# Turning the attention probabilities with plain products against a scaled diagonal

## The chip, the cores and the metric

One Trainium2 chip; the program runs on one of its cores. The metric is the device time of one execution in microseconds (us), here the median of the timed runs.

## The reference

The model is two transformer blocks over 512 latent and 256 context tokens of width 1024, everything in float32. What the change touches are its two attentions. Both compute softmax(scale · Q Kᵀ) V per head:

```python
def attend(q, k, v):                       # first block (MLA): 8 heads, 512 queries, 768 keys, value width 128
    s = jnp.einsum('bqhd,bkhd->bhqk', q, k).astype(F32) * MLA_SCALE
    p = jax.nn.softmax(s, axis=-1).astype(v.dtype)
    return jnp.einsum('bhqk,bkhd->bqhd', p, v)

# second block (GQA): 8 query heads in 2 groups, 512 queries, 512 keys, head width 64
scores = jnp.einsum('bqkgd,bskd->bkgqs', qblk, k).astype(jnp.float32) * scale
p = jax.nn.softmax(scores, axis=-1).astype(v.dtype)
return jnp.einsum('bkgqs,bskd->bqkgd', p, v)
```

## The kernel before

The program is a row of stages (`build`, from L3796). Each stage is a block with one instruction stream for each engine; the engines meet through semaphores, and the next stage starts when all are through. The stages with the attentions are reached from `mla` (call at L2662: 8 heads, key segments of 256 and 512, so 768 keys) and from `second_mixer` (call at L3247: 8 heads, 512 keys). They are called the MLA attention and the GQA attention below.

Float32 products are mostly made in three passes (`three_passes`, L300 to L305; L303, L304 and L305 are the three matmuls): each operand is held as a rounded high part and a low part, both of the type float32r, and high·high, high·low and low·high are added up in PSUM. A plain float32 product (`nc.tensor.matmul` on float32 operands) is one instruction in the source.

`attention` (L2271) serves both calls. Its work is cut into 32 units u = (head h, query block a of 128 queries), all written out (no loop on the engines). For a unit:

- TensorE, `score(u)`, L2316: scores of 128 queries against all keys, into a PSUM score bank. MLA: 10 matmuls (5 with 256 and 5 with 512 keys); GQA: 3 matmuls of 512 keys with 64 rows (the head width).
- VectorE, `find_peak(u)`: the row maximum (L2393) and its product with minus the scale (L2394).
- ScalarE, `raise_(u)`, L2359: exp of the scores, from PSUM into the buffer `probs` in SBUF, with the row sum as a by-product.
- VectorE: reciprocal of the row sum (L2412), then the whole probability tile times that share, in place (L2413), which releases `normed`.
- TensorE, L2342: each block of 128 queries x 128 keys is transposed against the identity `ident` into a PSUM bank (6 blocks in MLA, 4 in GQA), which releases `t_done`.
- ScalarE, `high(u)`, L2366: rounds the turned tile into a high part; VectorE, `low(u)`, L2399: the rest, which releases `t_kept`.
- TensorE, `value(m, part)`, L2328 (the matmuls are recorded at L303 to L305): probabilities times values for a pair of units; one half of the key blocks goes behind each unit (9 matmuls a unit in MLA, 6 in GQA, each 256 wide).
- ScalarE L2371 and VectorE L2405 split the output of a pair.

The order on each engine is the order in the source. TensorE, for every u: score(u+2); wait for `normed` of u; wait for `t_kept` of the unit that used the turn bank before; the transpositions of u; then half a `value` of the pair before. VectorE, for every u: wait for `raised` of u, L2412, L2413, low(u-1), every second time out_low, find_peak(u+2). ScalarE: high(u-1), every second time out_high, raise_(u+1). There are two `probs` buffers; MLA has 2 score banks and 1 turn bank (L2661), GQA has 3 score banks and 2 turn banks (L3246). Neither attention moves any data by DMA.

`k.row` is a scratch row of 768 words per partition; `stats` takes its words 0 to 31, and the GQA side keeps `steps` in words 704 to 767.

Of the kernel before, what the change touches and what calls it, by code (L numbers as in the profile page):

```python
# [28 lines left out]
ALU = mybir.AluOpType  # L29
AX = mybir.AxisListType  # L30

P = 128
# [267 lines left out]
def three_passes(k, out, stationary, moving, start, stop, **more):  # L300

    (sh, sl), (mh, ml) = stationary, moving
    k.nc.tensor.matmul(out, sh, mh, start=start, stop=False, **more)  # L303
    k.nc.tensor.matmul(out, sh, ml, start=False, stop=False, **more)  # L304
    return k.nc.tensor.matmul(out, sl, mh, start=False, stop=stop, **more)  # L305
# [1965 lines left out]
def attention(k, heads, key_segs, products_of, value_of, out_rows, dst_of, scale, rooms):  # L2271

    nc = k.nc
    k.stage()
    lo = key_segs[0][0]
    width = T - lo
    tiles = width // P
    stats = k.row[:, 0:32].rearrange("p (b c) -> p b c", c=4)  # L2280
    units = [(h, a) for h in range(heads) for a in range(4)]
    n_units, n_pairs, ahead = len(units), len(units) // 2, rooms.ahead
    probs, turned = rooms.probs, rooms.turned
    n_probs, n_scores, n_turns = len(probs), len(rooms.score_banks), len(rooms.turn_banks)
    names = ("scored", "peak", "raised", "normed", "t_done", "t_high", "t_kept", "o_done", "o_high", "o_kept")
    scored, peak, raised, normed, t_done, t_high, t_kept, o_done, o_high, o_kept = (k.sem(s) for s in names)

    def scores(u):
        return rooms.score_banks[u % n_scores]

    run = probs[0].shape[2]

    def probs_block(u, b):
        at = b * P % run
        return probs[u % n_probs][:, b * P // run, at:at + P]

    def turn_bank(u):
        return rooms.turn_banks[u % n_turns]

    def out_bank(m):  # L2300
        return rooms.out_banks[m % 2][:, 0:2 * P]

    def out(m):
        return out_bank(m)[out_rows(m // 2), :]

    with k.block() as block:
        @block.tensor
        def _(pe):
            def score(u):
                if u >= n_scores:  # L2310
                    pe.wait_ge(raised, u - n_scores + 1)
                h, a = units[u]
                for t0, n in key_segs:
                    products = products_of(h, a, t0, t0 + n)
                    for i, (queries, keys) in enumerate(products):
                        last = nc.tensor.matmul(scores(u)[:, t0 - lo:t0 - lo + n], queries, keys, start=i == 0,  # L2316
                                                stop=i == len(products) - 1)
                last.then_inc(scored, 1)

            def value(m, part):  # L2320
                h = m // 2
                if part == 0:
                    pe.wait_ge(t_kept, 2 * m + 2)
                    if m >= 2:
                        pe.wait_ge(o_kept, m - 1)
                half = tiles // 2
                for b in range(part * half, part * half + half):
                    last = three_passes(k, out_bank(m), value_of(h, b), turned[m % 2].tokens(b, 0, 2 * P),  # L2328
                                        b == 0, b == tiles - 1)
                if part:  # L2330
                    last.then_inc(o_done, 1)

            for u in range(ahead):
                score(u)
            for u in range(n_units):
                if u + ahead < n_units:
                    score(u + ahead)
                pe.wait_ge(normed, u + 1)
                if u >= n_turns:
                    pe.wait_ge(t_kept, u - n_turns + 1)  # L2340
                for b in range(tiles):
                    last = nc.tensor.transpose(turn_bank(u)[:, b * P:(b + 1) * P], probs_block(u, b), k.const("ident"))  # L2342
                last.then_inc(t_done, 1)
                if u >= 2:
                    value(u // 2 - 1, u % 2)
            for part in range(2):
                value(n_pairs - 1, part)

        def turned_part(part, u):
            at = P * (u % 2)  # L2350
            return part[:, :, at:at + P]

        @block.scalar
        def _(act):
            def raise_(u):
                act.wait_ge(peak, u + 1)
                if u >= n_probs:
                    act.wait_ge(t_done, u - n_probs + 1)
                nc.scalar.activation(probs[u % n_probs], scores(u).rearrange("p (c t) -> p c t", t=run), ACT.Exp, scale=scale,  # L2359
                                     bias=stats[:, u % 8, 1:2], accum_out=stats[:, u % 8, 2:3]).then_inc(raised, 1)  # L2360

            def high(u):
                act.wait_ge(t_done, u + 1)
                if u % 2 == 0 and u >= 4:
                    act.wait_ge(o_done, u // 2 - 1)
                nc.scalar.copy(turned_part(turned[u // 2 % 2].high, u),  # L2366
                               turn_bank(u).rearrange("p (b q) -> p b q", q=P)).then_inc(t_high, 1)

            def out_high(m):
                act.wait_ge(o_done, m + 1)  # L2370
                nc.scalar.copy(dst_of(m // 2, m % 2)[0], out(m)).then_inc(o_high, 1)  # L2371

            for u in range(ahead - 1):
                raise_(u)
            for u in range(n_units):
                if u:
                    high(u - 1)
                if u >= 4 and u % 2 == 0:
                    out_high(u // 2 - 2)
                if u + ahead - 1 < n_units:  # L2380
                    raise_(u + ahead - 1)
            high(n_units - 1)
            for m in range(n_pairs - 2, n_pairs):
                out_high(m)

        @block.vector
        def _(dve):
            chain = Chain(dve, k.sem("chain"))

            def find_peak(u):  # L2390
                dve.wait_ge(scored, u + 1)
                b = u % 8
                chain.link(nc.vector.tensor_reduce(stats[:, b, 0:1], scores(u), AX.X, ALU.max))  # L2393
                nc.vector.tensor_scalar(stats[:, b, 1:2], stats[:, b, 0:1], -scale, None, ALU.mult).then_inc(peak, 1)  # L2394

            def low(u):
                dve.wait_ge(t_high, u + 1)
                pair = turned[u // 2 % 2]
                nc.vector.tensor_tensor(turned_part(pair.low, u), turn_bank(u).rearrange("p (b q) -> p b q", q=P),  # L2399
                                        turned_part(pair.high_plain, u), ALU.subtract).then_inc(t_kept, 1)  # L2400

            def out_low(m):
                dve.wait_ge(o_high, m + 1)
                high, high_plain, low = dst_of(m // 2, m % 2)
                nc.vector.tensor_tensor(low, out(m), high_plain, ALU.subtract).then_inc(o_kept, 1)  # L2405

            for u in range(ahead):
                find_peak(u)
            for u in range(n_units):
                dve.wait_ge(raised, u + 1)  # L2410
                b = u % 8
                chain.link(nc.vector.reciprocal(stats[:, b, 3:4], stats[:, b, 2:3]))  # L2412
                nc.vector.tensor_scalar(probs[u % n_probs], probs[u % n_probs], stats[:, b, 3:4], None,  # L2413
                                        ALU.mult).then_inc(normed, 1)
                if u:
                    low(u - 1)
                if u >= 4 and u % 2 == 0:
                    out_low(u // 2 - 2)
                if u + ahead < n_units:
                    find_peak(u + ahead)  # L2420
            low(n_units - 1)
            for m in range(n_pairs - 2, n_pairs):
                out_low(m)
# [204 lines left out]
def mla(k, norm):  # L2628
# [28 lines left out]
    def dst_of(h, half):  # L2657
        t = slice(2 * P * half, 2 * P * half + 2 * P)
        return qn.high[:, h, t], qn.high_plain[:, h, t], qn.low[:, h, t]

    rooms = AttentionRooms(probs, turned, [k.pair(0), k.pair(1)], [k.pair(2)], [k.bank(6), k.bank(7)], 2)  # L2661
    attention(k, MLA_HEADS, SEGS, products_of, lambda h, b: v.tokens(b, h * P, (h + 1) * P), lambda h: slice(0, P),  # L2662
              dst_of, MLA_SCALE, rooms)
    project_residual(k, "mla_w_o", qn, 2, SEG_LAT, k.mod_next)
# [1336 lines left out]
```

## Time and profile before

| | us |
|---|---|
| median of 2 runs | 3065.28 (3064.45 to 3066.12) |
| the profiled execution | 3065.66 |
| its span in the trace | 3063.8 |
| MLA attention, first score to the start of the last value products | 1457 to 1574 |
| GQA attention, the same | 2307 to 2385 |

The profiled execution lies 1.9 us above its span (work around the span) and 0.4 us above the median of the runs. PE is TensorE's matmuls, PEld its weight loads, DVE VectorE, ACT ScalarE. The duration of a matmul in the trace holds its way through the array, so matmuls overlap one another: what one costs is the distance from its start to the next start. In the timeline view a merged row of n like instructions gives the first start and the time from there to the end of the last.

### The profile page before, as it was taken

The page shows a single profiled execution, that of the slowest core. Times are in us where ns is not written, and L with a number is a line of the kernel's source. Part 1 is how long each engine was busy: PE and PEld are TensorE (multiplying, and loading weights), DVE is VectorE, ACT ScalarE, POOL GpSimd, SP SyncE. Part 2 cuts the span into 40 slices and gives each one's busy share as a digit, 9 for nine tenths or more (in the row PEclk, how much of TensorE's full clock was granted, in tenths as well). Part 3 has the DMA queues.
Part 4 walks back from the last instruction along what each step waited for, and adds up shares of the span by engine and source line. Part 5 has one row for each costly group of instructions (what it writes and reads, how often), then busy time and mean ns, then how long its engine had stood idle before and what let it go on. Part 6 is the DMA issues. An engine that isn't in the chain of part 4 may idle for free. (4 is left out here: it accounts for less than half of the span.)

```text
span 3063.8 us, 37588 instructions
## 1 busy us (share of the span) xinstructions
PE 2832.1 (92%) x14082; PEld 2298.8 (75%) x14082; DVE 1716.9 (56%) x2444; ACT 1221.6 (40%) x1627; POOL 180.4 (6%) x160
## 2 busy tenths in 40 slices
PE   7999989799999999898999999989979989899998
PEld 3864877688888898786887887867756667777776
DVE  3764553645677453526854433351258564788887
ACT  4210323323332242423534443243426422577776
POOL 0000001100011000000000000000000000122221
PEclk9999989899999999999999999999988999999999
DMA  5500330122345142112012221212200024799996
GB/s 232 180 21 14 119 102 1 35 89 69 123 141 178 65 161 94 61 31 63 1 49 89 103 90 69 99 57 85 86 15 1 1 69 166 284 366 358 354 354 220
DMA packets 79612, 359.71 MB, mean 117 GB/s; under 512 B 13570, under 2 KB 18467, under 8 KB 54788
## 3 DMA queue, kind: packets, MB, share of 16 engines
q1 hardware_dynamic: 61348, 307.74, 28.1%
q0 software_dynamic: 18144, 50.36, 5.4%
q8 instruction: 76, 1.25, 0.2%
q14 instruction: 44, 0.36, 0.0%
HBM read 356.47 MB, written 16.25 MB: 122 GB/s over the span
## 5 line engine op out<-in xcount | busy, mean ns | idle before, releaser
L303 PE MATMUL ps<-rounded,rounded 128*128 128x512 f32 (+2 forms) x3540 | 1302.5, 368 | 113.5 <-DVEq L1090 19.1
L304 PE MATMUL ps<-rounded,rounded 128*128 128x512 f32 (+2 forms) x3540 | 1282.0, 362 | 0.0
L305 PE MATMUL ps<-rounded,rounded 128*128 128x512 f32 (+2 forms) x3540 | 1280.9, 362 | 0.0
L303 PEld LDWEIGHTS ps<-rounded,rounded 128*128 128x128 f32 (+1 forms) x3540 | 677.8, 191 | 235.5 <-issue 75.2
L305 PEld LDWEIGHTS ps<-rounded,rounded 128*128 128x128 f32 (+1 forms) x3540 | 676.5, 191 | 103.2
L304 PEld LDWEIGHTS ps<-rounded,rounded 128*128 128x128 f32 (+1 forms) x3540 | 678.3, 192 | 96.3
L282 DVE TENSOR_TENSOR rounded<-work,rounded 128x1024 fp32r<-128x1024 f32 (+3 forms) x224 | 306.4, 1370 | 744.3 <-ACT rounded L278 744.0
L278 ACT CAST rounded<-work 128x1024 fp32r<-128x1024 f32 (+3 forms) x224 | 260.7, 1166 | 709.8 <-PE ps L305 601.7
L3749 DVE TENSOR_TENSOR rounded<-work,rounded 128x2048 fp32r<-128x2048 f32 x138 | 309.9, 2287 | 70.9 <-ACT rounded L3569 70.9
L3569 ACT CAST rounded<-work 128x2048 fp32r<-128x2048 f32 x138 | 258.9, 1912 | 74.2 <-PE ps L305 74.2
L289 PE MATMUL ps<-cst 128*128 128x256 f32 x530 | 141.1, 425 | 35.6 <-PEq L169 35.6
L289 PEld LDWEIGHTS ps<-cst 128*128 128x128 f32 x530 | 111.8, 216 | 59.7 <-issue 42.5
L278 ACT ACT_TABLE_LOAD x34 | 43.6, 1283 | 192.4 <-PE ps L305 183.7
L493 DVE SCALAR_TENSOR_TENSOR work<-work,silu_c 128x256 f32<-128x256 f32 x224 | 103.7, 484 | 12.6 <-DMA work<-in_ada_w 6.7
L2316 PE MATMUL ps<-rounded,rounded 128*128 128x256 f32 (+2 forms) x416 | 95.8, 370 | 5.6 <-PEq L169 5.1
L1173 ACT ACTIVATE work<-work 128x768 f32<-128x768 f32 (+1 forms) x44 | 32.5, 739 | 126.6 <-DVE work L1208 126.6
L1086 DVE SCALAR_TENSOR_TENSOR work<-ps,vec,work 128x255 f32<-128x255 f32 (+3 forms) x116 | 72.5, 654 | 15.9 <-ACT work L1056 11.9
L3447 POOL DMA_INDIRECT out_x<-h,whole x23 | 60.4, 2627 | 349.0 <-ACT h L3611 349.0
L2316 PEld LDWEIGHTS ps<-rounded,rounded 128*128 128x128 f32 (+1 forms) x416 | 64.8, 195 | 18.8 <-issue 7.9
L2366 ACT CAST rounded<-ps 128x768 fp32r<-128x768 f32 (+1 forms) x64 | 44.4, 694 | 67.6 <-PE ps L2342 67.5
L1486 PE MATMUL ps<-work 128*128 128x512 f32 x160 | 71.2, 604 | 0.0
L918 DVE SCALAR_TENSOR_TENSOR work<-work,silu_c 128x512 f32<-128x512 f32 x98 | 67.7, 747 | 6.0 <-DMA work<-in_ada_w 4.3
(509 smaller groups left out, 2484.8 us busy)
## 6 DMA issues: line engine op xcount, KB each, us to landing
work<-in_moe SPq DMA_DIRECT2D x138, 1024.0 KB, 7.8
work<-in_ffn_up SPq DMA_DIRECT2D x44, 1024.0 KB, 4.8
work<-in_ada_w POOLq DMA_DIRECT2D x80, 512.0 KB, 4.1
work<-in_ffn_down SPq DMA_DIRECT2D x66, 512.0 KB, 3.4
work<-in_ada_w SPq DMA_DIRECT2D x4, 2048.0 KB, 23.5
work<-in_w_out SPq DMA_DIRECT2D x16, 512.0 KB, 3.4
work<-in_w_gates SPq DMA_DIRECT2D x16, 512.0 KB, 3.5
work<-in_w_in_hy SPq DMA_DIRECT2D x12, 512.0 KB, 4.5
```

The costliest lines, as they stand in the source:

```text
L278: self.k.nc.scalar.copy(self.parts[s][0], self.raw[s]).then_inc(self.rounded[s], 1)
L282: self.k.nc.vector.tensor_tensor(self.parts[s][1], self.raw[s], self.high_plain[s], ALU.subtract).then_inc(self.ready[s], 1)
L289: k.nc.tensor.matmul(k.bank(bank, 2 * P), k.const("ident"), k.cst[:, 0:2 * P], start=True, stop=True)
L303: k.nc.tensor.matmul(out, sh, mh, start=start, stop=False, **more)
L304: k.nc.tensor.matmul(out, sh, ml, start=False, stop=False, **more)
L305: return k.nc.tensor.matmul(out, sl, mh, start=False, stop=stop, **more)
L493: done = self.k.nc.vector.scalar_tensor_tensor(out=total, in0=tile, scalar=by, in1=total, op0=ALU.mult, op1=ALU.add)
L1086: nc.vector.scalar_tensor_tensor(out=out, in0=k.pair(p)[:, lo + o:hi + o], scalar=k.col(conv_w, n + tiles * (o + taps // 2)), in1=out, op0 ...
L1486: last = nc.tensor.matmul(bank(group, part), tab[part][:, a, n * P:(n + 1) * P], src[:, a, :], start=a == 0, stop=a == count - 1)
L2316: last = nc.tensor.matmul(scores(u)[:, t0 - lo:t0 - lo + n], queries, keys, start=i == 0, stop=i == len(products) - 1)
L3569: nc.scalar.copy(ring.parts[:, c % ring.SPLIT, 0, :], ring.raw[c % ring.RAW]).then_inc(ring.rounded, 1)
L3749: V.tensor_tensor(ring.parts[:, s, 1, :], ring.raw[c % ring.RAW], ring.plain[:, s, 0, :], ALU.subtract).then_inc(ring.ready, 1)
```

## The change

The probabilities stay unscaled. VectorE scales the 128x128 identity with the row's shares (the reciprocals) into one of three small tiles `shares`, and TensorE turns each block by a plain float32 product of the block (stationary) with that diagonal (moving), which turns and scales in one. VectorE's write of a `shares` tile waits for the unit three before to be turned. Nothing else is changed.

```diff
     stats = k.row[:, 0:32].rearrange("p (b c) -> p b c", c=4)
+    shares = [k.row[:, 64 + P * i:64 + P * (i + 1)] for i in range(3)]
...
                 for b in range(tiles):
-                    last = nc.tensor.transpose(turn_bank(u)[:, b * P:(b + 1) * P], probs_block(u, b), k.const("ident"))
+                    last = nc.tensor.matmul(turn_bank(u)[:, b * P:(b + 1) * P], probs_block(u, b), shares[u % 3], start=True, stop=True)
                 last.then_inc(t_done, 1)
...
                 chain.link(nc.vector.reciprocal(stats[:, b, 3:4], stats[:, b, 2:3]))
-                nc.vector.tensor_scalar(probs[u % n_probs], probs[u % n_probs], stats[:, b, 3:4], None,
-                                        ALU.mult).then_inc(normed, 1)
+                if u >= 3:
+                    dve.wait_ge(t_done, u - 2)
+                nc.vector.tensor_scalar(shares[u % 3], k.const("ident"), stats[:, b, 3:4], None, ALU.mult).then_inc(normed, 1)
```

## Rows read from the trace of the kernel before

**Rows 1.** Windows, MLA: window, length, busy us PE, PEld, DVE, ACT, POOL, PEclk, DMA.
```profile
1480.00:1560.00 80.00, 80.00 (x578) 74.01 (x575) 68.18 (x128) 43.42 (x81) 0.00 (x0) 1.00 0.00 1
```
**Rows 2.** Timeline of the MLA attention: one unit, from transposition to transposition.
```profile
1483.22 0.82 PE L2342 MATMUL ps<-cst,x 128*128 128x128 f32 x6
...
1483.79 0.36 PE L303 MATMUL ps<-rounded,rounded 128*128 128x256 f32 x1
...
1484.08 0.80 ACT L2366 CAST rounded<-ps 128x768 fp32r<-128x768 f32 x1 [1.15 <-PE ps L2342]
...
1486.70 0.49 PE L2342 MATMUL ps<-cst,x 128*128 128x128 f32 x3
```
**Rows 3.** The windows view again, the steady part of the GQA attention and its start.
```profile
2330.00:2380.00 50.00, 49.92 (x298) 37.34 (x296) 48.00 (x126) 34.15 (x79) 0.00 (x0) 1.00 0.00 1
2306.00:2322.00 16.00, 14.84 (x43) 10.31 (x44) 10.36 (x26) 7.01 (x15) 0.00 (x0) 0.50 0.00 0
```
**Rows 4.** Timeline of the GQA attention: two steady units.
```profile
2342.68 0.49 DVE L2413 TENSOR_SCALAR work<-work,row 128x512 f32<-128x512 f32 x1
...
2343.35 0.66 PE L2342 MATMUL ps<-cst,work 128*128 128x128 f32 x4
...
2344.65 0.96 PE L2316 MATMUL ps<-rounded,rounded 64*128 64x512 f32 x3
2344.66 0.48 DVE L2413 TENSOR_SCALAR work<-work,row 128x512 f32<-128x512 f32 x1
...
2345.54 0.66 PE L2342 MATMUL ps<-cst,work 128*128 128x128 f32 x4
```
**Rows 5.** All instructions of L2342: durations in ns, min/median/max.
```profile
L2342 PE MATMUL ps<-cst,x x192: 272/272/302, 1463.2 to 1569.9; 128*128 128x128 f32 x192
L2342 PE MATMUL ps<-cst,work x128: 272/273/476, 2311.3 to 2382.4; 128*128 128x128 f32 x128
```
**Rows 6.** Timeline: plain 128-wide float32 products (L1906), 4 in the source.
```profile
499.61 1.16 PE L1906 MATMUL ps<-work 128*128 128x128 f32 x8 [0.24 <-ACT work L2060]
```
**Rows 7.** Timeline: plain float32 products of 129 columns at full clock.
```profile
556.83 0.39 PE L2003 MATMUL ps<-work 128*128 128x129 f32 x2
557.05 0.39 PE L2000 MATMUL ps<-work 128*128 128x129 f32 x2
```
**Rows 8.** Timeline of the MLA attention: its first three turns.
```profile
1463.24 0.82 PE L2342 MATMUL ps<-cst,x 128*128 128x128 f32 x6
...
1465.36 0.94 DVE L2399 TENSOR_TENSOR rounded<-ps,rounded 128x768 fp32r<-128x768 f32 x1
...
1466.44 0.85 PE L2342 MATMUL ps<-cst,x 128*128 128x128 f32 x6 [0.63 <-DVE rounded L2399]
...
1469.27 0.85 PE L2342 MATMUL ps<-cst,x 128*128 128x128 f32 x6 [0.22 <-DVE rounded L2399]
```
**Rows 9.** Timeline of the GQA attention: its first turn, and the third.
```profile
2311.34 1.12 PE L2342 MATMUL ps<-cst,work 128*128 128x128 f32 x4 [0.29 <-DVE work L2413]
...
2316.58 1.11 PE L2342 MATMUL ps<-cst,work 128*128 128x128 f32 x4
2317.34 0.56 PE L303 MATMUL ps<-rounded,rounded 128*128 128x256 f32 x1
```
**Rows 10.** Timeline: plain float32 products of 129 columns at half clock.
```profile
549.23 0.64 PE L2000 MATMUL ps<-work 128*128 128x129 f32 x2
549.66 0.64 PE L2003 MATMUL ps<-work 128*128 128x129 f32 x2
```
**Rows 11.** Timeline of the GQA attention: the next to last turn.
```profile
2380.47 0.66 PE L2342 MATMUL ps<-cst,work 128*128 128x128 f32 x4 [0.51 <-DVE work L2413]
```
**Rows 12.** VectorE, groups by shape: the scaling in each attention, and a 128-column one.
```profile
L2413 DVE TENSOR_SCALAR x<-x,row 128x768 f32<-128x768 f32 x32 | 24.1, 753 | 1.1
...
L2413 DVE TENSOR_SCALAR work<-work,row 128x512 f32<-128x512 f32 x32 | 15.6, 487 | 1.1
...
L3064 DVE TENSOR_SCALAR rounded<-cst 128x128 fp32r<-128x128 f32 x2 | 0.4, 222 | 0.0
```

## The prediction

> **What bounds the kernel now.** I read first the windows view over the two attentions, to see which engine is full; then the timeline of one unit, to get the distance from one turn to the next and what fills it; then the same for products of the new kind elsewhere in the program. In the steady MLA attention TensorE is busy 80.0 of 80 us, with the full clock granted (2.4 GHz), VectorE 68.2 [rows 1]. Busy matmuls overlap, so the starts have to be looked at: turns begin at 1483.22 and 1486.70, 3.48 us apart, and I counted the same 3.48 between 27 successive turns; the six transpositions take 0.57 of it (to the start of L303), products and scores follow with no gap [rows 2]. Nothing jitters: this is TensorE's own pace. In the GQA attention it is less plain, for VectorE is busy 48.0 of 50 us beside TensorE's 49.9 [rows 3]. The turns are 2.19 us apart (2343.35 to 2345.54). VectorE's scaling ends at 2343.17 in one unit and at 2345.14 in the next, 0.18 and 0.40 us ahead of the turn, and yet the turn begins 0.89 us after the start of its scores in both (from 2344.65 to 2345.54, and 25 units of the timeline show it to 0.01 us) [rows 4]. A releaser that moves by 0.2 us without moving the turn isn't what releases it. So TensorE sets the pace here as well, with VectorE some 0.05 to 0.2 us behind. Both attentions stand alone between block boundaries, with no transfer to hide or expose, so each microsecond on TensorE goes to the end.
>
> **A transposition and a plain product.** L2342 has 320 matmul records, 192 and 128, which is 32 units by 6 and by 4: one record for one transposition [rows 5]. Six of them span 0.82 us, the last lasting 0.27, so the starts are (0.82 - 0.27)/5 = 0.109 us apart [rows 2]. A plain float32 product of the same 128x128 form stands at L1906: 4 products in the source are 8 records, two for each. Their span gives (1.16 - 0.275)/7 = 0.126 a record, with the first one after a wait in it, 0.25 a product [rows 6]. In a longer run, products of 129 columns come at 556.83 and 557.05, 0.22 us for one product in two records, 0.1117 a record to the nanosecond [rows 7]. So one plain product costs from 0.22 to 0.25 us against 0.109. The turns stand in a full stream, as the run of rows 7 does, so I take 0.223: 0.114 more for each block. Half a record less on either side is not seen anywhere. The floor of the range is a product made in one record like a transposition (0.00 more), the ceiling 0.14 more, from rows 6.
>
> The Trainium skill has two rules on this. Its page FP8 and Floating Point Precision (TensorE Precision Notes) says that true float32 takes four passes through the array, its page TensorE: Matmul & The Clock Gate (Back-to-back issue gap) gives 81 ns as the sustained spacing of a 128-column matmul beside its weight load. Taken alone, the second would make the new turn cheaper than the old (an estimate, 320 x (0.081 - 0.109) = -9 us); by the first an estimate is 4 x 128 columns at 2.4 GHz = 0.213 us, which the 0.22 of the trace bears out. The trace's spacing decides.
>
> **MLA, step by step.** A steady unit gets 6 x 0.114 = 0.69 us longer: 3.48 to 4.17. Do other loops take over? With one turn bank the loop turn, high, low, next turn is: 6 plain products 11 x 0.1117 + 0.275 = 1.50, ScalarE 0.80, VectorE 0.94, and 0.2 of signals, 3.46 us [rows 2, 8]. That is under 4.17, so the steady units don't feel it, 27 x 0.69 = 18.5. It decides where no scores or no values stand beside the turn: the first two distances are 3.20 (1463.24 to 1466.44) and 2.83 now, with VectorE's low as the releaser [rows 8]; they become 3.46 each, and the last two, the same pair within 0.01, likewise: 2 x (0.26 + 0.63) = 1.8. The last turn adds its own 0.69. Sum 21.0 us.
>
> **GQA.** A steady unit gets 4 x 0.114 = 0.457 longer: 2.19 to 2.65, for 25 units 11.4 us. The first four units run at half clock (1.2 GHz granted over all of 2306 to 2322) [rows 3]. A turn takes 0.76 us there (2316.58 to 2317.34) [rows 9], a plain product of 129 columns 0.43 (549.23 to 549.66, in a stretch at half clock) [rows 10], so 4 x 0.43 - 0.76 = 0.95 more, four times 3.8. The last three turns, at full clock, add 1.4 but give back the 0.51 for which the next to last one waits for VectorE's queue [rows 11], 0.9 net. The first turn stops waiting 0.29 for L2413 [rows 9]. Sum 3.8 + 11.4 + 0.9 - 0.3 = 15.8.
>
> **VectorE's side.** L2413 falls from 0.753 and 0.487 us to about the 0.222 of a 128-column one (L3064): 32 x 0.53 + 32 x 0.27 = 25.5 us less busy [rows 12]. It is worth the 0.8 us counted above and no more: in the steady units TensorE doesn't wait for it. Were TensorE's surcharge gone, the most to be had is that plus VectorE's nearness in GQA, under 0.1 us a unit. The new wait on `t_done` is for the turn three units back; before it, in the same queue, stands low(u-2), which needs the turn of u-2 to be done, so it is always met: cost 0 (at worst an instruction's handling, 29 times on an engine with slack). Behind it are low and find_peak. The smaller tiles take words 64 to 447 of the scratch row, which no other part of these stages uses. ScalarE's release of `probs` by `t_done` comes 0.46 to 0.69 us later, but its exp already stands behind high(u), which waits for a later turn.
>
> **Sum.** 21.0 + 15.8 = 36.8 us on the profiled 3065.66, 3102.5; against the median, 0.4 lower, 3102. That is 1.2% slower, inside the 2% that a measurement of this kernel can tell from no change.
>
> **Rivals.**
> 1. *The clock comes back earlier in GQA.* Half clock is granted for 16 us of it although TensorE works through [rows 3]; the MLA attention never has it [rows 1]. If plain products change what the grant follows, the low stretch is shorter. Price: each of the first four units, 3.6 us at half clock (2.62 now for the first two, half of 2311.34 to 2316.58 [rows 9], plus 0.95), would be nearer 2.65; two or three units earlier, minus 2 to 3, and with the whole gone minus 6: 3096 to 3100, say 3098. The skill's clock page (Part 4, PE-mode transpose) says that transpositions don't count as activity in the same way, which speaks for it; the MLA attention, at full clock with 0.57 of 3.48 us in transpositions, neither shows nor refutes it.
> 2. *A product is dearer here*: 0.25 as at L1906, for the weights come from a buffer that ScalarE writes and the moving diagonal from one that VectorE writes. 320 x 0.027 = 9 more: 3111.
> 3. *Not slower: one record for a product.* If a product against the diagonal came out as one record of 0.11, TensorE's pace would stay and the waits of rows 9 and 11 fall out: minus 0.8 us, 3064. It decides below 0.1115 us a product (320 x 0.0025 = 0.8). Against it: all plain products of rows 6, 7 and 10 have two records.
> 4. *Slower by over 2%*: the clock falls to half in the attentions, as it did at 549 with TensorE in full work [rows 10]. MLA units at half clock near 7.5 us, 32 x 3.4 = 110 more: 3210. Against it: TensorE gets denser, not idler.
>
> **Chances.** Forecast 0.55, rival 1 0.27, rival 2 0.12, rival 3 0.03, rival 4 0.03. The range takes in 1 and most of 2: low 3094, high 3111. Faster by over 2% needs 61 us, more than anything that this change touches on VectorE's path: 0.01. Slower by over 2%: 0.03, rival 4. The rest, 0.96, is within 2%.
>
> **What would show it.** Right: L2342 has 640 matmul records, 0.112 apart; MLA turns 4.17 us apart and GQA turns 2.65; L2413's successor lasts about 0.22; TensorE still has no gap in the middle of either; VectorE falls from 68 to near 46 busy us in 80. Wrong: 320 records; turns closer than 4.0 in MLA; a new wait ahead of L2342 in steady units; half clock anywhere in 1457 to 1600; any stage outside the two attentions that moves by over 2 us.

## The result and the profile after

| | before | changed |
|---|---|---|
| median of 2 runs, us | 3065.28 | 3110.45 (3109.40 to 3111.51) |
| ratio, 95% interval | | 1.0138 (1.0111 to 1.0164) |
| the profiled execution's span, us | 3063.8 | 3109.7 |

So 45 us more, where 37 were forecast: slower, within 2%, inside the stated range by half a microsecond. Timed again, five runs beside 17 of the kernel before (e5 below), the changed kernel comes out at 1.0118 (1.0099 to 1.0137) of 3070.8, which is 36 us. In microseconds the two intervals are 34 to 50 and 30 to 42.

The page of the changed kernel, its first lines:

```profile
span 3109.7 us, 38286 instructions
## 1 busy us (share of the span) xinstructions
PE 2874.5 (92%) x14402; PEld 2343.3 (75%) x14402; DVE 1702.7 (55%) x2444; ACT 1220.9 (39%) x1627; POOL 182.8 (6%) x160
```

TensorE has 320 records more than before (14082 then), VectorE the same number. VectorE's busy time (1716.9 before) fell by only 14 us, less than the 25.5 forecast: the scaling itself fell by 24.1 + 15.6 - 18.4 = 21.3, but where instructions overlap in the trace the busy time counts them once, and there was more such overlap before. All instructions of the turning line (L2343 now), durations in ns, then the start of the first and of the last; and VectorE's new scaling:

```profile
L2343 PE MATMUL ps<-row,x x384: 270/275/348, 1464.4 to 1592.5; 128*128 128x128 f32 x192
L2343 PE MATMUL ps<-row,work x256: 273/275/581, 2338.5 to 2426.5; 128*128 128x128 f32 x128
```
```profile
L2416 DVE TENSOR_SCALAR row<-cst,row 128x128 f32<-128x128 f32 x64 | 18.4, 287 | 2.3
```

These two answer to [rows 5] and [rows 12]. There are 640 records where 320 stood: each plain product is two. The distance from the first to the last start is the best ruler for a whole attention, since it holds every turn and everything between them and nothing outside. MLA: 128.1 us against 1569.9 - 1463.2 = 106.7 before, 21.4 more. GQA: 88.0 against 71.1, 16.9 more. Both ends are printed to 0.1 us, so each reading is good to 0.1. Together 38.3; the other 7 of the 45 us stand in stages that the change doesn't touch, most of it between the two attentions (from the last turn of MLA to the first of GQA 741.4 us before, 746.0 here).

The windows view over the steady middle of both (window, length, busy us of PE, PEld, DVE, ACT, POOL, granted clock, DMA), to lay beside [rows 1] and [rows 3]:

```profile
core 0: us, PE busy (x) PEld busy (x) DVE busy (x) ACT busy (x) POOL busy (x), PEclk, DMA share, GB/s
1490.00:1570.00 80.00, 80.00 (x597) 75.86 (x596) 49.20 (x105) 36.13 (x67) 0.00 (x0) 1.00 0.00 1
2360.00:2420.00 60.00, 60.00 (x381) 47.71 (x380) 46.50 (x124) 32.99 (x79) 0.00 (x0) 1.00 0.00 1
```

TensorE is full as before; VectorE fell from 68 to 49 busy us in 80, and nobody is the faster for it. The timeline of one MLA unit:

```profile
1488.23 1.50 PE L2343 MATMUL ps<-row,x 128*128 128x128 f32 x12
...
1489.48 0.36 PE L303 MATMUL ps<-rounded,rounded 128*128 128x256 f32 x1
...
1489.68 0.29 DVE L2416 TENSOR_SCALAR row<-cst,row 128x128 f32<-128x128 f32 x1
...
1489.77 0.80 ACT L2367 CAST rounded<-ps 128x768 fp32r<-128x768 f32 x1 [1.83 <-PE ps L2343]
...
1490.60 0.96 DVE L2400 TENSOR_TENSOR rounded<-ps,rounded 128x768 fp32r<-128x768 f32 x1 [0.63 <-ACT rounded L2367]
...
1492.40 0.38 PE L2343 MATMUL ps<-row,x 128*128 128x128 f32 x2
```

Turns are 4.17 us apart (3.48 in [rows 2]); the turn takes 1.25 us where it took 0.57. ScalarE's and VectorE's halves of the loop end at 1491.56, 0.84 us before the next turn: it is not what the turn waits for. Two GQA units:

```profile
2373.70 1.16 PE L2343 MATMUL ps<-row,work 128*128 128x128 f32 x8
...
2374.61 0.36 PE L303 MATMUL ps<-rounded,rounded 128*128 128x256 f32 x1
...
2376.38 1.16 PE L2343 MATMUL ps<-row,work 128*128 128x128 f32 x8
```

2.68 to 2.69 us apart (2.19 in [rows 4]).

### The profile page after: what moved, and what is told of

Same layout as the page of the kernel before. It is cut to its first block and busy times, and to the rows that moved or that the text cites. A ratio compares the mean times of both kernels' runs of the same rounds, so it can differ in the third digit from the quotient of the medians.

```text
span 3109.7 us, 38286 instructions
## 1 busy us (share of the span) xinstructions
PE 2874.5 (92%) x14402; PEld 2343.3 (75%) x14402; DVE 1702.7 (55%) x2444; ACT 1220.9 (39%) x1627; POOL 182.8 (6%) x160
## 5 line engine op out<-in xcount | busy, mean ns | idle before, releaser
L2400 DVE TENSOR_TENSOR rounded<-ps,rounded 128x768 fp32r<-128x768 f32 (+1 forms) x64 | 52.8, 825 | 40.8 <-ACT rounded L2367 40.8
L2394 DVE TENSOR_REDUCE row<-ps 128x1 f32<-128x768 f32 (+1 forms) x64 | 52.8, 825 | 36.5 <-PE ps L2317 36.3
```

## The experiments

In all of them the ruler is the one above. Its readings come from the row of the turning instructions in each profile:

| run | time, ratio to before (95%) | MLA, first to last start, us | GQA |
|---|---|---|---|
| before | | 106.7 | 71.1 |
| changed | 1.0138 (1.0111 to 1.0164) | 128.1 | 88.0 |
| e1 MLA only | 1.0071 (1.0051 to 1.0090) | 128.1 | 72.9 |
| e2 GQA only | 1.0038 (1.0024 to 1.0052) | 106.6 | 86.2 |
| e3 relief only | 0.9994 (0.9976 to 1.0012) | 105.8 | 69.3 |
| e4 plain products only | 1.0110 (1.0071 to 1.0149) | 128.1 | 86.0 |
| e5 changed again | 1.0118 (1.0099 to 1.0137) | 128.1 | 86.1 |
| e6 float32r diagonal | 1.0130 (1.0109 to 1.0152) | 106.1 | 118.0 |
| e7 products at the start of GQA | 0.9976 (0.9963 to 0.9990) | 106.7 | 66.9 |
| e8 float32r in MLA only | 1.0001 (0.9988 to 1.0013) | 106.1 | 71.0 |
| e9 e6 with early products | 1.0148 (1.0131 to 1.0165) | 106.2 | 118.4 |
| e10 early products | 1.0011 (1.0002 to 1.0021) | 106.6 | 73.3 |
| e11 e6 with e7's products | 0.9998 (0.9986 to 1.0010) | 106.2 | 67.4 |
| e12 e7 again | 0.9994 (0.9979 to 1.0008) | 106.7 | 67.0 |

The kernel before was timed beside each group of these runs. Its times scatter from 3060 to 3080, with medians of 3065 to 3071; a difference under about 4 us needs both the interval and the ruler.

### e1 and e2: one attention at a time

In e1 the new turn and the new scaling stand under `if tiles == 6`, in e2 under `if tiles == 4`, with the old ones in the other branch (the line for the turn shown, for e1):

```diff
+                    if tiles == 6:
                         last = nc.tensor.matmul(turn_bank(u)[:, b * P:(b + 1) * P], probs_block(u, b), shares[u % 3], start=True, stop=True)
+                    else:
+                        last = nc.tensor.transpose(turn_bank(u)[:, b * P:(b + 1) * P], probs_block(u, b), k.const("ident"))
```

> Only the MLA attention is changed; GQA is as before. Theory A (TensorE's pace sets both attentions, a plain product costs 0.114 us more per block): MLA turns 4.17 us apart, the MLA stage 21.5 us longer, GQA turns stay 2.19 apart; time before + 21 to 23 us. Theory B (the 7 us that the profile of the changed kernel shows outside the attentions comes with the change, by its shift of later stages or its longer instruction stream): about half of it here too, before + 25. If it is scatter between executions, the sum of this run's excess and that of the GQA-only one lies near 38, not 45.

> Only the GQA attention is changed. Theory A: GQA turns 2.69 us apart, the GQA stage 16 to 17 us longer, MLA turns stay 3.48 apart; time before + 16 to 17. Theory B (stages outside the attentions lengthen too): before + 20. Rival (the diagonal's gain on VectorE pays for part of it in GQA): before + 8 or less.

Measured: 0.71% and 0.38% of 3067.6, 22 and 12 us (24 and 15 by the medians). Their sum is 33, with the two half widths of 6 and 4 us; it holds 38 and lies well below 45. The ruler has +21.4 in MLA for e1 and +15.1 in GQA for e2, with the other attention at 106.6 in e2, as before, and at 72.9 in e1, 1.8 above before. GQA's code in e1 is that of before; what differs is how long its half clock lasts (five turns come at it, four before), and that is the scatter of this reading. Timelines of e1 in MLA, then of e2 in GQA:

```profile
1500.87 1.50 PE L2344 MATMUL ps<-row,x 128*128 128x128 f32 x12
1505.04 1.50 PE L2344 MATMUL ps<-row,x 128*128 128x128 f32 x12
```
```profile
2349.80 1.16 PE L2344 MATMUL ps<-row,work 128*128 128x128 f32 x8
2352.49 1.16 PE L2344 MATMUL ps<-row,work 128*128 128x128 f32 x8
2355.18 1.16 PE L2344 MATMUL ps<-row,work 128*128 128x128 f32 x8
```

4.17 and 2.69, as in the changed kernel: the costs add up, and neither depends on the other.

### e3 and e4: the relief alone, the plain products alone

e3 keeps VectorE's diagonals and turns against the identity, so the output lacks the scaling by the shares. e4 keeps the scaling in place and turns with plain products against the identity.

```diff
 e3, against the changed kernel
-                    last = nc.tensor.matmul(turn_bank(u)[:, b * P:(b + 1) * P], probs_block(u, b), shares[u % 3], start=True, stop=True)
+                    last = nc.tensor.transpose(turn_bank(u)[:, b * P:(b + 1) * P], probs_block(u, b), k.const("ident"))
 e4, against the kernel before
-                    last = nc.tensor.transpose(turn_bank(u)[:, b * P:(b + 1) * P], probs_block(u, b), k.const("ident"))
+                    last = nc.tensor.matmul(turn_bank(u)[:, b * P:(b + 1) * P], probs_block(u, b), k.const("ident"), start=True, stop=True)
```

> The blocks are turned by transpositions against the identity as before, VectorE makes the diagonals but nothing reads them, so the scaling by the shares is left out of the output. Only VectorE's relief is left. Theory A: VectorE falls by about 21 busy us, the MLA turns stay 3.48 and the GQA turns 2.19 apart, time before - 0.5 to - 1.5 (the waits at the two ends of GQA). Rival (VectorE sets the pace in GQA, where it was busy 48.0 of 50 us): before - 5 to - 8.

> VectorE scales the probabilities in place as before, but the blocks are turned by plain products against the identity. Theory A: the whole loss without the relief: MLA turns 4.17, GQA turns 2.69 apart, time as the changed kernel's or up to 1.5 us above it (before + 45 to + 47). Rival (the dearer part comes from the diagonal as the moving operand, or from its signals): turns closer than 4.10 in MLA, before + 30 or less.

e3 is level with before within its interval, which reaches down to -7 us and so doesn't exclude the rival by itself. The ruler finds 0.9 us less in MLA and 1.8 less in GQA, and the timeline shows the steady turns as far apart as they were, with VectorE done early. Windows of e3, then one diagonal and its turn:

```profile
1480.00:1560.00 80.00, 80.00 (x577) 74.02 (x576) 58.26 (x127) 43.05 (x80) 0.00 (x0) 1.00 0.01 1
2330.00:2378.00 48.00, 47.93 (x287) 35.95 (x286) 43.88 (x122) 32.50 (x77) 0.00 (x0) 1.00 0.00 1
```
```profile
2342.36 0.29 DVE L2416 TENSOR_SCALAR row<-cst,row 128x128 f32<-128x128 f32 x1
...
2343.46 0.66 PE L2343 MATMUL ps<-cst,work 128*128 128x128 f32 x4
```

The diagonal is ready at 2342.65, 0.8 us ahead of the turn, and the turns still come 2.19 us apart (2341.27 to 2343.46). That settles the doubtful point of the forecast: VectorE at 96% busy in GQA did not set the pace of the steady units. It was as close as the forecast said: in the kernel before, two of the 25 steady distances are 2.27 and 2.29 us instead of 2.19, and both times the scaling ends only 0.05 to 0.06 us ahead of the turn, which then begins 0.97 or 0.99 us after its scores and not 0.89. The first of the two:

```profile
2355.61 0.96 PE L2316 MATMUL ps<-rounded,rounded 64*128 64x512 f32 x3
2356.03 0.49 DVE L2413 TENSOR_SCALAR work<-work,row 128x512 f32<-128x512 f32 x1
...
2356.58 0.66 PE L2342 MATMUL ps<-cst,work 128*128 128x128 f32 x4
```

In e3 both are 2.19: 0.2 us in all. e4 has the whole loss (34 us by its runs, on the ruler 128.1 and 86.0, as e5 to 0.1), so the diagonal as the moving operand, its signals and the new wait cost nothing that can be seen, and the relief on VectorE returns nothing that can be seen once TensorE is slower. The 45 to 47 us expected of e4 were the first timing's 45 and fell with it. e4's interval, 22 to 46 us, is wide (4 runs); the ruler carries this reading.

### e5: the changed kernel again

> The changed kernel itself, timed again beside the kernel before, and profiled a second time. If the 7 us that its first profile shows outside the attentions are scatter between executions, the ratio comes nearer 1.012 (+ 37 us) and the stages outside the attentions stand otherwise in the second profile; if they come with the change, the ratio stays at 1.0145 and they stand the same. The MLA stage + 21.5, GQA + 15 to 17 in both cases.

36 us, and the ruler has 21.4 and 15.0, together 36.4. The first profile's 7 us outside the attentions are not there a second time: this span is 3098.9, 35.1 above that of before. So they were scatter between executions; where it comes from was not taken apart. From the last turn of MLA to the first of GQA it is 739.7 us this time, 1.7 less than before, where the first profile had 4.6 more, and e1 has 4.5 more as well with GQA's code unchanged. The half clock at the start of GQA scatters too, and there it changes the ruler. From e5:

```profile
2325.00:2340.00 15.00, 14.69 (x46) 11.16 (x46) 7.66 (x21) 6.61 (x14) 0.00 (x0) 0.50 0.01 2
2341.00:2360.00 19.00, 19.00 (x121) 15.00 (x119) 14.33 (x39) 10.04 (x24) 0.00 (x0) 1.00 0.00 1
```
```profile
2336.65 2.07 PE L2343 MATMUL ps<-row,work 128*128 128x128 f32 x8
...
2341.25 1.16 PE L2343 MATMUL ps<-row,work 128*128 128x128 f32 x8
```

Three turns come at half clock here (a turn of 2.07 us), the fourth already at full clock (1.16 us); in the first profile it was four turns, and 88.0 on the ruler instead of 86.1. The two runs of the first timing gave 45 us for a cost that lies near 36 to 38.

### e6: one record a product

Both operands in float32r: exp writes rounded probabilities, the diagonal is rounded, into tiles that each attention hands over (a less precise result than the plain product's).

```diff
-    probs = [k.x[:, 3 * b:3 * b + 3, 0:CTX] for b in range(2)]
+    spare = k.rounded(X_AT, DT, T)
+    probs = [spare[:, 3 * b:3 * b + 3, 0:CTX] for b in range(2)]
+    shares = [spare[:, 6, 0:P], spare[:, 6, P:2 * P], spare[:, 7, 0:P]]
...
-    probs = [k.words(WORK_AT + b * LAT, WORK_AT + (b + 1) * LAT).rearrange("p (c t) -> p c t", t=LAT)
+    probs = [k.rounded_words(WORK_AT + b * LAT, WORK_AT + (b + 1) * LAT).rearrange("p (c t) -> p c t", t=LAT)
              for b in range(2)]
+    shares = [k.rounded_words(WORK_AT + 2 * LAT + b * P, WORK_AT + 2 * LAT + (b + 1) * P) for b in range(3)]
```

> The change with both operands of the turning product in float32r: exp writes rounded probabilities, and VectorE rounds the diagonal; less precise than the plain product. Theory A (what costs is the second record of each product, not the product as such): 320 records, 0.11 to 0.12 us apart, MLA turns 3.48 to 3.54 apart, GQA turns 2.19 to 2.23 apart, time before - 1 to + 2. Rival (a product against the diagonal is dear in any type): MLA turns above 4.0, before + 30 or more.

In MLA it is theory A: 192 records, turns 3.49 apart, 106.1 on the ruler. (The records are a little closer than expected: six in 0.78 us, the last lasting 0.27, are 0.10 apart.) In GQA there are also 128 records, one for each block, but the ruler reads 118.0, and the time is 40 us up. Neither theory had this. Windows of e6, and the turns in both attentions:

```profile
1480.00:1560.00 80.00, 80.00 (x575) 75.06 (x574) 57.56 (x127) 43.40 (x82) 0.00 (x0) 1.00 0.01 1
2330.00:2420.00 90.00, 90.00 (x295) 68.33 (x295) 47.52 (x125) 33.23 (x79) 0.00 (x0) 0.50 0.00 1
```
```profile
1501.57 0.78 PE L2343 MATMUL ps<-rounded 128*128 128x128 f32 x6
1505.06 0.79 PE L2343 MATMUL ps<-rounded 128*128 128x128 f32 x6
...
2353.20 1.11 PE L2343 MATMUL ps<-rounded,rounded 128*128 128x128 f32 x4
2357.21 1.11 PE L2343 MATMUL ps<-rounded,rounded 128*128 128x128 f32 x4
```

The granted clock is 0.50 (1.2 GHz) over all of 2330 to 2420, with TensorE busy 90 us of 90, and a unit takes 4.01 us. The kernel before enters GQA at half clock too, but has the full clock (1.00 from 2330 on [rows 3]). That raised three questions: does the float32r product lose the clock anywhere (e8), would it hold the full clock if it had it (e9, e11), and is there something to be had in the kernel before (e7, e10, e12)?

### e8: float32r in MLA alone

> The float32r product with the diagonal in the MLA attention alone; GQA as in the kernel before (transpositions, scaling in place). In the run with both, MLA turns came 3.49 us apart with the full clock and the whole loss stood in GQA, at half clock. If that reading is right: MLA turns 3.49 apart, GQA as before with the clock back after 13 to 17 us, time before - 1 to + 1. Rival (float32r products take the clock wherever they stand, MLA had luck): half clock inside 1460 to 1570, before + 20 or more.

1.0001: MLA 106.1 as in e6, GQA 71.0 as before, so the reading of e6 is right. The float32r product costs nothing in MLA and doesn't take the clock from it. It gains about half a microsecond there, too little to see in the times.

### e7, e10 and e12: products to raise the clock, in the kernel before

e7 and e12 put 4 plain products of 256 columns, whose result nobody reads, behind the first scores of GQA (`keep_running`; its numbers are the count and the PSUM bank); e10 puts 3 behind the last product of the stage ahead and 1 behind the first scores.

```diff
 e7, e12
             for u in range(ahead):
                 score(u)
+            if tiles == 4:
+                keep_running(k, 4, 3)
```

> The kernel before with 4 plain products of 256 columns (8 records, results unused) put into TensorE's wait for the first probabilities of the GQA attention. Theory C (the clock stays at half there because TensorE waits before the first turn and then runs scores with 64 rows): full clock is granted at least one unit earlier, half clock after 2306 falls from 16 us to 9 to 13, time before - 1 to - 4. Rival (the clock follows something else, or the added products delay the first turn): low stretch unchanged, time before + 0 to + 3.

> The kernel before with the same 3 + 1 plain products. Against the run with 4 products behind the first scores, which held TensorE for 3.4 us there, these lie mostly in a wait of 3.4 us at the end of the stage ahead. Theory C: half clock ends by 2312 of the profile, time before - 3 to - 6. Rival (the clock comes back no earlier, or the products hold up the first scores): before - 2 to + 2.

> The kernel before with 4 plain products behind the first scores of GQA, timed a second time, since its first interval (0.9963 to 0.9990) is near the scatter of the runs. If the gain is real, the ratio is below 1 again, 0.996 to 0.999 (before - 3 to - 12), and half clock at the start of GQA is again some 10 us shorter than the 27.3 of the kernel before. If it was scatter, 0.999 to 1.001.

Windows of e7, then of e10:

```profile
2302.00:2309.00 7.00, 6.19 (x14) 4.33 (x14) 2.75 (x7) 2.84 (x5) 0.00 (x0) 0.50 0.00 0
2310.00:2320.00 10.00, 9.48 (x53) 6.63 (x53) 9.43 (x26) 6.63 (x15) 0.00 (x0) 1.00 0.01 2
```
```profile
2303.00:2330.00 27.00, 26.44 (x71) 16.71 (x70) 18.48 (x41) 12.00 (x25) 0.00 (x0) 0.50 0.00 1
2331.00:2340.00 9.00, 9.00 (x55) 6.76 (x55) 8.49 (x22) 5.99 (x14) 0.00 (x0) 1.00 0.00 1
```

Four in one run behind the first scores bring the full clock back by 2310, in time for the first turn; the ruler falls by 4.2 us in e7 and 4.1 in e12. But they stand ahead of the first turn, outside the ruler. From the timeline of e7, then of the kernel before:

```profile
2302.81 2.89 PE L2316 MATMUL ps<-rounded,rounded 64*128 64x512 f32 x6 [3.42 <-PEq L169]
...
2305.63 3.66 PE L289 MATMUL ps<-cst 128*128 128x256 f32 x8
...
2310.11 0.66 PE L2344 MATMUL ps<-cst,work 128*128 128x128 f32 x4
```
```profile
2306.88 4.17 PE L2316 MATMUL ps<-rounded,rounded 64*128 64x512 f32 x9 [3.42 <-PEq L169]
```

In e7 the first turn comes 7.30 us after the first score, against 4.46 before (2306.88 to 2311.34 [rows 9]), so 2.8 of the 4.2 go back. That leaves 1.4 us. The first timing gave 0.24% (7 us), the second 0.06% with an interval that holds no change: the gain isn't shown. With three of the same products a little earlier and only one behind the scores (e10) the clock comes back no sooner, 0.50 up to 2330, and the kernel is a little slower (0.11%).

### e9 and e11: the same, with the float32r diagonal

> The float32r products in both attentions, with 3 plain products behind the last one of the stage ahead of the GQA attention (where TensorE waits for VectorE and ScalarE) and 1 behind its first scores. Theory C (the clock is lost ahead of GQA and not found again by this mix, but it would hold once it is there, as it holds in MLA): full clock within the first units of GQA and to its end, GQA turns 2.19 to 2.25 apart, time before - 2 to - 5. Rival (the mix of 64-row scores and float32r turns itself takes the clock away): half clock returns inside the attention, before + 20 or more.

> The float32r products in both attentions, with all 4 plain products behind the first scores of GQA, the place that brought the full clock back within 3 us in the kernel before. Reading 1 (this mix can't raise the clock but keeps it): full clock from the first units to the end of GQA, turns 2.19 to 2.25 us apart, time before - 3 to + 1. Reading 2 (this mix loses the clock too): it rises and falls back to half inside the attention, before + 20 or more.

e9 stays at half clock throughout, as e6. e11, with the four products in one place, has it:

```profile
2330.00:2370.00 40.00, 40.00 (x234) 30.21 (x233) 35.82 (x98) 26.26 (x64) 0.00 (x0) 1.00 0.00 1
```
```profile
2340.16 0.66 PE L2345 MATMUL ps<-rounded,rounded 128*128 128x128 f32 x4
2342.40 0.66 PE L2345 MATMUL ps<-rounded,rounded 128*128 128x128 f32 x4
2344.64 0.66 PE L2345 MATMUL ps<-rounded,rounded 128*128 128x128 f32 x4
```

Reading 1 holds for the profiled execution: full clock to the end, turns 2.24 apart, 67.4 on the ruler. It took 3069 us, and seven more of the 11 timed runs 3060 to 3069. The other three took 3113 to 3117 us, e6's time, and the clock granted to them on average is 0.944 to 0.947, e6's 0.945 to 0.947, where the eight have 0.962 to 0.965. So these three most likely stayed at half clock through GQA, though there is no trace of one. The ratio, 0.9998, is that of the eight. So this version doesn't beat the kernel before, and can't be relied on.

## Why the prediction was right

- *What bounds the kernel.* Right in both attentions. For MLA nothing else was in sight; for GQA the argument from [rows 4], that a releaser which moves by 0.2 us without moving the turn isn't the releaser, was tested by e3 and held. The 0.89 us that it gives for 25 units holds in 24 of 26; in the other two VectorE was the releaser and cost 0.2 us together.
- *A plain product at 0.223 us.* Right: 12 records in 1.50 us give (1.50 - 0.275)/11 = 0.111 a record, two a product. e4 shows that it is the product as such, with any moving operand; e6 and e8, that it is the second record: with one, MLA's turns are back at 3.49. (The floor of "0.00 more" that stands there would be a time like that of before, which is rival 3; the range as stated starts at 3094, a little under rival 1.)
- *MLA, 21.0 us.* Measured 21.4 in all four profiles that have it, with steady turns at 4.17 and the end pieces at 3.47 and 3.55 for the 3.46 forecast (its terms add up to 3.44).
- *GQA, 15.8 us.* Measured 16.9, 15.0, 15.1 and 14.9 (changed, e5, e2, e4). On the ruler the forecast is 16.1, since the wait of 0.3 us ahead of the first turn lies outside it. That it is met so closely is in part luck, for two terms are off in opposite directions. The steady unit was undersized: 2.69, not 2.65, for the turn takes 0.91 us (2373.70 to 2374.61), 0.50 more than the 0.41 of before and not 0.457; the 25 steady distances came to 12.3 us more, not 11.4. The half-clock start was counted in units, four of them, 3.8 us. The changed kernel's first profile has four turns there (4.1 us more), but e5, e2 and e4 have three: the half clock lasts 13 to 20 us of the attention with either kind of turn (the shortest in e3), and fewer of the longer units fit in. In e5 that part is 2.2 us.
- *VectorE's relief.* That it is worth 0.8 us was too low for the relief alone. e3 has 2.7 on the ruler: 0.9 at the ends of MLA, where low(u-1) stands behind the scaling, which the forecast had not counted; in GQA 0.4 at the last two turns and 0.2 in the two units above. The other 1.1 us stand in the third and fourth distance of GQA (3.90 and 3.14 before, 3.73 and 2.19 in e3), where the half clock ended sooner, and that scatters without any change (e1). Ahead of the ruler, the first turn of GQA comes 4.26 us after the first score, 4.46 before: 0.2, where 0.3 was counted. In the changed kernel the relief counts for nothing that can be seen (e4 against e5).
- *The small tile.* It takes 0.287 us, not the 0.222 of L3064 in [rows 12], and so VectorE fell to 49 busy us in 80 and not to 46. L3064 was the wrong row: it combines a matrix with two constants and writes float32r. An instruction like the new one, the identity times a column of numbers, float32 in and out, stood in the kernel before at 283 ns:

```profile
L435 DVE TENSOR_SCALAR h<-cst,made 128x128 f32<-128x128 f32 x16 | 3.4, 283 | 0.1
```

- *Sum.* 36.8 forecast, 36 measured by e5; the 45 of the first timing holds some 9 us that didn't come again, 2 of them in GQA's half clock and 7 outside the attentions. The 7 are a stated sign of being wrong (a stage outside that moves by over 2 us): it did show, in the first profile, and e5 answers it. That the first timing lies inside the range says little, since by half a microsecond more it would not; the spacings and the ruler carry the forecast.
- *Rival 1, the clock comes back earlier in GQA.* Fell. From the first score it is 16 us to the full clock before and in e5, 20 in the first profile of the changed kernel, and 20 in e1 with transpositions. One turn fewer at half clock, as in e5, is worth 1.9 us (88.0 against 86.1); the 6 us set down for all four don't follow from the rival's own units (4 x 0.95 = 3.8). The first profile of the changed kernel, with four turns at half clock:

```profile
2334.00:2354.00 20.00, 19.66 (x63) 15.12 (x64) 9.63 (x26) 7.29 (x16) 0.00 (x0) 0.50 0.01 1
```

- *Rival 2 (0.25 us a product)* gives 3111, and the first timing alone, 3110.45, would have spoken for it; it fell by the spacing, 0.111 a record. *Rival 3 (one record)* fell by the count, and e6 shows what it would have been. *Rival 4 (half clock in an attention, slower by 2% and more)* didn't happen to this change, but its mechanism is real: e6 and e9 have it over nearly the whole GQA attention, at 47 us.

## What to carry to other kernels

A plain float32 product against an identity or a diagonal is not a transposition with a factor for free: it is two records where the transposition is one, 0.223 against 0.109 us for 128x128. Moving work off an engine that is 96% busy brought next to nothing here where another one was at 100%, and a share of busy time doesn't tell which of two nearly full engines decides; whether the turn follows its supposed releaser from unit to unit does. And where two executions a side give a difference of 1%, time the pair again before explaining its last quarter: the sum over the stages that a change touches was steadier than the whole here (38.3, then 36.4, where the spans gave 45.9, then 35.1).

## What the runs showed that was not expected

The same 128x128 blocks, turned in the same places, leave GQA at different clocks. With transpositions (before) and with plain products (changed, e4) the full clock comes back after 15 to 20 us of the attention; with one-record float32r products (e6, e9) it stays at half for nearly all of it, with TensorE busy 90 us of 90, which turned an even change into 40 us lost. In MLA the same products keep the full clock that is there (e8). Four plain products in one run, at the right place, brought the clock back before the first turn (e7, e12) and let the float32r version keep it (e11). A rule of the Trainium skill (TensorE: Matmul & The Clock Gate, Part 4, PE-mode transpose) has it that transpositions don't engage the full clock, as they don't count as busy in the same way. These traces show the opposite order: the attention with transpositions regains the full clock (0.50 over 2306 to 2322, 1.00 from 2330 on [rows 3]) and the one with ordinary float32r products of as many columns doesn't (0.50 over 2330 to 2420 in e6). Transpositions are only 4 of the 13 products of a unit there, so this says nothing of transpositions alone. What in the mix decides it was not settled here.
